# Hybrid stage re-laid: two sets of recurrence buffers, clamp as Relu, grouped ScalarE functions, output blocks in another order

## The reference, cut to what matters

```
x : 1 x 256 tokens x 1024 float32, two layers
per layer i:  h += 0.5 * SwiGLU_1(RMSNorm(h))          # d_ff 2816
              h += Mixer_i(RMSNorm(h))                 # layer 0: hybrid, layer 1: differential attention
              h += 0.5 * SwiGLU_2(RMSNorm(h))
hybrid: z, xbc, dt, gate, x_b = split(hn @ hyb_w_in)
  SSD:  xbc = silu(conv4(xbc));  dt = softplus(dt + bias);  cs = cumsum(dt * a) in chunks of 128
        y = sum_j (C_i.B_j) exp(cs_i - cs_j) dt_j x_j  (j <= i) + state of the chunk before + d * x
        y = rms_norm_in_2_groups(y * silu(z))
  LRU:  xb = conv4(x_b);  r = sigmoid(xb @ w_ra + b);  i = sigmoid(xb @ w_ix + b)
        a = exp(-8 r softplus(-lambda));  h_t = a h_(t-1) + sqrt(1 - a^2) i xb;  out = gelu(gate) * h
  h += concat(y, out) @ hyb_w_out
attention: q, k, v = split(hn @ w_qkv); rope; softmax(q1 k1) - lam softmax(q2 k2); per-head norm; @ w_o
```

## Time and profile before

| | |
|---|---|
| median of 3 runs | 1081.09 us (1081.01 to 1081.24) |
| the profiled execution's own time | 1081.11 us |
| its span, first to last instruction | 1079.3 us |
| mean granted TensorE clock | 0.988 |
| PE busy | 1054.2 us (98%) |
| PEld busy | 949.0 us (88%) |
| DVE busy | 807.9 us (75%) |
| ACT busy | 614.2 us (57%) |
| POOL busy | 69.2 us (6%) |
| hybrid stage (first input block to the next stage's first block) | 195.84 to 395.86 us of the span |
| attention stage | 765.3 to 885.2 us of the span |

### The profile page before, as it was taken

The page is one execution under the profiler, slowest core; times in us unless marked ns, Lnnn a source line. Parts: engine busy times, 40 slices in busy tenths (PEclk is TensorE's granted clock), DMA queues, the critical chain, the costliest instruction groups (busy, mean ns, idle before and its releaser), DMA issues. The chain is left out here.

```text
span 1079.3 us, 18474 instructions
## 1 busy us (share of the span) xinstructions
PE 1054.2 (98%) x6669; PEld 949.0 (88%) x6669; DVE 807.9 (75%) x1141; ACT 614.2 (57%) x982; POOL 69.2 (6%) x80
## 2 busy tenths in 40 slices
PE   9999999998988999999999999999999999999997
PEld 8888888897888998888888888888989998888886
DVE  6888775799898758888656888766689578888753
ACT  6555543676887555555534555544455756555541
POOL 0200011100131000000011000002100000000021
PEclk9999999998988999999999999999999999999999
DMA  9866676556443656667764666775475437666671
GB/s 253 215 192 190 197 215 170 141 152 204 117 123 102 178 160 191 194 193 209 195 189 142 190 190 191 222 195 166 120 203 158 126 100 213 192 189 196 190 206 39
DMA packets 365602, 189.07 MB, mean 175 GB/s; under 512 B 5840, under 2 KB 364512, under 8 KB 365552
## 3 DMA queue, kind: packets, MB, share of 16 engines
q1 hardware_dynamic: 365296, 187.84, 61.6%
q0 software_dynamic: 256, 0.59, 0.3%
HBM read 186.81 MB, written 1.06 MB: 174 GB/s over the span
## 5 line engine op out<-in xcount | busy, mean ns | idle before, releaser
L190 DVE TENSOR_TENSOR wlo<-raw,whi 128x1024 fp32r<-128x1024 f32 (+1 forms) x324 | 419.8, 1315 | 67.9 <-ACT whi L185 66.3
L185 ACT ACTIVATE whi<-raw 128x1024 fp32r<-128x1024 f32 (+1 forms) x322 | 352.1, 1114 | 26.5 <-PE psum L205 19.9
L217 PE MATMUL psum<-xn,whi 128*128 128x512 f32 x1408 | 354.4, 393 | 0.1
L217 PEld LDWEIGHTS psum<-xn,whi 128*128 128x128 f32 x1408 | 253.5, 189 | 45.9 <-DVE xn L302 0.4
L220 PEld LDWEIGHTS psum<-xn,wlo 128*128 128x128 f32 x1408 | 192.4, 190 | 13.8
L220 PE MATMUL psum<-xn,wlo 128*128 128x256 f32 x1408 | 196.9, 282 | 0.0
L217 PE MATMUL psum<-hid,whi 128*128 128x512 f32 x704 | 171.8, 391 | 0.0
L217 PEld LDWEIGHTS psum<-hid,whi 128*128 128x128 f32 x704 | 128.1, 189 | 24.0
L201 PE MATMUL psum<-xn,whi 128*128 128x256 f32 x480 | 124.1, 295 | 0.7 <-ACT arena L1530 0.7
L202 PE MATMUL psum<-xn,whi 128*128 128x256 f32 x480 | 121.2, 288 | 0.0
L505 ACT ACTIVATE arena<-arena 128x256 f32<-128x256 f32 x88 | 36.9, 420 | 112.1 <-DVE arena L558 112.1
(11 more groups left out here) (218 smaller groups left out, 913.6 us busy)
## 6 DMA issues: line engine op xcount, KB each, us to landing
raw<-in_ffn_gate SPq DMA_DIRECT2D x88, 512.0 KB, 3.9
raw<-in_ffn_up SPq DMA_DIRECT2D x88, 512.0 KB, 3.9
raw<-in_ffn_down SPq DMA_DIRECT2D x64, 704.0 KB, 4.6
raw<-in_hyb_w_in SPq DMA_DIRECT2D x36, 512.0 KB, 4.3
raw<-in_dif_w_qkv SPq DMA_DIRECT2D x24, 512.0 KB, 4.6
raw<-in_hyb_w_out SPq DMA_DIRECT2D x16, 512.0 KB, 4.3
raw<-in_dif_w_o SPq DMA_DIRECT2D x8, 512.0 KB, 4.3
hid<-cs_rows SPq DMA_DIRECT2D x4, 512.0 KB, 6.7
```

The costliest lines, as they stand in the source:

```text
L185: act.activation(whi[:, s, 0:k * P], raw[:, s, 0:k * P], ACT.Copy).then_inc(s_whi, 1)
L190: dve.tensor_tensor(wlo[:, s, 0:k * P], raw[:, s, 0:k * P], whi[:, s, 0:k * P].bitcast(F32), ALU.subtract).then_inc(s_wlo, 1)
L217: pe.matmul(acc, hi[:, j, :], x[:, t, :, :], start=start and j == 0, stop=False)
```

## The change

The hybrid stage and its neighbours are edited so:

- **dt** is turned to tokens first; softplus runs on 128 x 32; the cumulative sums come from TensorE (`sums_of_dt`, five matmuls against the triangle, between the two blocks of pair 5) in place of VectorE's scans. The heads' bias and a are spread by one matmul. The softplus of the LRU's lambda moves into the down products of the FFN before.
- **Decays**: ScalarE clamps (four `Relu` of 128 columns with a bias per partition) and takes one exponential of 512 columns for a pair of heads. The block off the diagonal is a product of two factors: exp(cs) goes to DRAM and back as `erows` beside `csb`, and VectorE makes two products of 128 columns from it. `exponents` is gone; `decay_products` on the diagonal has 512 columns.
- **LRU** has two sets of buffers (the second in the place of the gates' weights and of xbc's B and C); the second half's sigmoids wait for all gate products of TensorE instead of for the scans. Functions of a kind are grouped on ScalarE. The scans of both halves run during the output blocks. The products on GpSimd move to VectorE (`lru_ix`, `gate_y`) and ScalarE (`square_y`).
- **x to tokens** goes in `after` 6, 7, 10, 12, on more banks; the group sums of both groups stand together after pair 16, and one `group_scales` stands between the blocks of pair 17.
- **Output** does all y blocks first and then all LRU blocks, with eight PSUM accumulators, and h is updated during the last eight blocks. The hand-over to the next stage goes by single blocks.
- VectorE no longer rounds the second block of pairs 15 and 16.
- **Attention**: the first `take_qk` comes before pair 2's rounding, lambda's exponential two steps later, and the third root before the second `output_hi`.

```diff
+        def begin_hi(act, p0, k, before, ring_full=True):
+            for b, left in zip(range(2 * p0, 2 * p0 + RING), before):
+                left(lambda: split_hi(act, b, b % RING, k, b // RING, ring_full))
...
-        lr, li, la = grid(10240, 4), grid(11264, 4), grid(12288, 4)
+        lr, li, la = (grid(10240, 4), grid(7168, 4)), (grid(11264, 4), grid(8192, 4)), (grid(12288, 4), xbc[:, 8:12, :])
...
         def gate_of(k):
...
-            return xbc[:, 8 + 2 * k:10 + 2 * k, :] if k < 2 else sz[:, 2 * k - 4:2 * k - 2, :]
+            return xtok[:, k % 2, 512 * (k // 2):512 * (k // 2) + 512].rearrange("p (m t) -> p m t", m=2)
...
-        OUT_BLOCKS = [(0, 0), (1, 0), (0, 1), (1, 1)] + [(d, q) for d in range(2, DT) for q in range(2)]
+        OUT_BLOCKS = [(d, q) for q in range(2) for d in range(DT)]
...
+        def out_sum(d):
+            return banks[(5, 7, 6, 4, 0, 1, 2, 3)[d]][:, 0:T]
...
                 if j == 18:
                     sp.wait_ge(s_cs, 1)
-                    sp.dma_start(cs_rows[:, :], cs).then_inc(s_csd, 16)
-                    sp.wait_ge(s_csd, 16)
+                    sp.dma_start(cs_rows[:, 0:T], cs).then_inc(s_csd, 16)
+                    sp.wait_ge(s_er, 1)
+                    sp.dma_start(cs_rows[:, T:T + P], dt_rows[:, 0:P]).then_inc(s_csd, 16)
+                    sp.wait_ge(s_csd, 32)
                 if j in (18, 20, 22, 24):
                     q = (j - 18) // 2
-                    rows = cs_rows[4 * q:4 * q + 4, :].unsqueeze(0).to_broadcast([P, 4, T])
...
                     sp.dma_start(csb[:, 4 * q:4 * q + 4, :], rows).then_inc(s_csb[q], 16)
+                    rows = cs_rows[4 * q:4 * q + 4, T:T + P].unsqueeze(0).to_broadcast([P, 4, P])
+                    sp.dma_start(erows[:, 4 * q:4 * q + 4, :], rows).then_inc(s_csb[q], 16)
...
+            def sums_of_dt():
+                pe.wait_ge(s_sp, 10)
+                for c in range(TC):
+                    pe.matmul(sum_rows[:, c * P:(c + 1) * P], DTA[:, c * HEADS:(c + 1) * HEADS], tri, start=True, stop=True)
+                pe.matmul(sum_tok[:, 0:2 * HEADS], tri, DTA, start=True, stop=True)
+                pe.matmul(sum_tok[:, 2 * HEADS:], tri, DTN[:, 0:HEADS], start=True, stop=False)
+                pe.matmul(sum_tok[:, 2 * HEADS:], ones, DTA[:, 0:HEADS], start=False, stop=True).then_inc(s_sums, 1)
             def c_dot_b():
...
+                mm.then_inc(s_cbp, 1)
             def x_to_tokens(g):
...
                 pe.wait_ge(s_xc, 6 + 2 * g)
-                if g >= 2:
-                    pe.wait_ge(s_xt, g - 1)
-                elif g == 1:
-                    pe.wait_ge(s_cb, 2)
+                if g == 2:
+                    pe.wait_ge(s_cb, 1)
+                    pe.wait_ge(s_cbo, 1)
+                elif g == 3:
...
                 if t == 0:
-                    pe.wait_ge(s_xt, 4)
-                if t >= 2:
-                    pe.wait_ge(s_gs, 2 * (t - 1))
-                o = banks[3 + t % 2]
+                    pe.wait_ge(s_cs, 1)
+                    pe.wait_ge(s_xt, 1)
+                elif t == 2:
+                    pe.wait_ge(s_xt, 2)
+                    pe.wait_ge(s_tok, 1)
...
+                    pe.wait_ge(s_gs, 2 * (t - 3))
+                o = banks[GATE_BANK[t % 4]]
...
             def group_sums(g):
...
             after = {s: [] for s in range(18)}
-            after[0] += [dt_product]
+            middle = {s: [] for s in range(18)}
+            after[0] += [dt_product, rows_of_heads]
+            after[2] += [dt_to_tokens]
+            middle[5] += [sums_of_dt]
             after[5] += [c_dot_b]
-            after[6] += [rows_to_tokens]
-            for g, s in enumerate((6, 7, 7, 8)):
+            for g, s in enumerate((6, 7, 10, 12)):
                 after[s] += [lambda g=g: x_to_tokens(g)]
             for m in range(8):
                 after[8 + m] += [lambda m=m: head_y(2 * m), lambda m=m: head_y(2 * m + 1)]
-            for k, s in enumerate((9, 10, 13, 14)):
+            for k, s in enumerate((9, 10, 12, 13)):
                 after[s] += [lambda k=k: lru_gates(2 * k), lambda k=k: lru_gates(2 * k + 1)]
-            after[14] += [lambda: group_sums(0)]
-            after[16] += [lambda: group_scale(0)]
-            after[16] += [lambda: group_sums(1)]
-            after[17] += [lambda: group_scale(1)]
+            after[16] += [lambda: group_sums(0), lambda: group_sums(1)]
+            middle[17] += [group_scales]
             for j in range(18):
                 read_out(pe, p0 + j - 2)
                 for m in range(2):
...
                 pe.wait_ge(s_ylo if t < 8 else s_blo, t % 8 + 1)
             for k, (d, q) in enumerate(OUT_BLOCKS):
-                if q == 0:
-                    read_out(pe, p0 + 16 + d)
+                if q == 0 and d in (4, 5):
+                    read_out(pe, p0 + 12 + d)
                 b = 2 * (p0 + 18) + k
-                multiply(pe, b, b % RING, DT, hid, 8 * q, half(p0 + 18 + d, 0), start=q == 0, stop=q == 1,
+                multiply(pe, b, b % RING, DT, hid, 8 * q, out_sum(d), start=q == 0, stop=q == 1,
                          need=ready if d == 0 else None)
...
+            def take_sums():
+                act.wait_ge(s_sums, 1)
+                act.activation(cs, sum_rows, ACT.Copy).then_inc(s_cs, 1)
+                act.activation(tok[:, 2 * HEADS:], sum_tok, ACT.Copy).then_inc(s_tok, 1)
+            def factors():
+                act.activation(dt_rows[:, 0:P], sum_rows[:, P:T], ACT.Exp).then_inc(s_er, 1)
+                act.wait_ge(s_tok, 1)
...
+            def decay(m):
+                act.wait_ge(s_csb[m // 2], 32)
+                act.wait_ge(s_tok, 1)
+                if m >= 2:
+                    act.wait_ge(s_y, 2 * m - 2)
+                if m == 5:
+                    act.wait_ge(s_tap, 3 * (NX + NL))
+                v = seg_pair(m)
+                for q in range(2):
+                    hd = 2 * m + q
+                    for c in range(TC):
+                        act.activation(v[:, q, 2 * P * c:2 * P * c + P], csb[:, hd, c * P:(c + 1) * P], ACT.Relu, scale=-1.0,
+                                       bias=tok[:, 32 + 16 * c + hd:33 + 16 * c + hd]).then_inc(s_seg, 1)
+                act.wait_ge(s_seg, 4 * m + 4)
+                d = diagonal(v)
+                act.activation(d, d, ACT.Exp, scale=-1.0).then_inc(s_dec, 1)
...
                 if t == 4:
-                    act.wait_ge(s_hl, 4)
-                o = banks[3 + t % 2]
...
-            todo[17] += [lambda: gelu(0), lambda: group_rms(0)]
-            todo[18] += [lambda: group_rms(1), lambda: mult_of_lru(1), lambda: gelu(1)]
-            todo[18] += [lambda: lru_hi(0)] + [lambda t=t: y_hi(t) for t in range(4)]
+            todo[3] += [softplus_exp]
+            todo[4] += [softplus_ln]
+            todo[7] += [take_cb_off]
+            for j in range(6):
+                todo[max(j + 3, 4)] += [lambda j=j: conv_silu(j)]
+            todo[6] += [take_sums]
+            todo[6] += [factors]
+            for m in range(8):
+                todo[8 + m] += [lambda m=m: decay(m)]
+            todo[12] += [lambda t=t: gates(t) for t in range(4)]
+            todo[13] += [lambda: decays_of_lru(0)]
+            todo[14] += [lambda t=t: gates(t) for t in range(4, 8)]
+            todo[15] += [lambda: decays_of_lru(1)]
+            todo[16] += [lambda: silu_z(0), lambda: silu_z(1)]
+            todo[17] += [lambda k=k: square_y(k) for k in range(4)]
+            todo[18] += [group_rms, lambda: mult_of_lru(0), lambda: mult_of_lru(1)]
+            todo[18] += [lambda t=t: y_hi(t) for t in range(4)]
             todo[19] += [lambda t=t: y_hi(t) for t in range(4, 8)]
-            todo[19] += [lambda: lru_hi(1), lambda: gelu(2), lambda: gelu(3)]
...
-            return [lambda: residual_hi(act, n + 1, DT - 2), lambda: residual_hi(act, n + 1, DT - 1)]
+            def left(d):
+                def work(split):
+                    split()
+                    residual_hi(act, n + 1, d)
+                return work
+            for d in range(4):
+                b = 2 * (p0 + 24) + d
+                left(d)(lambda: split_hi(act, b, b % RING, DT, b // RING))
...
             def decay_products(m):
-                dve.wait_ge(s_dec, 2 * m + 2)
-                v = seg_pair(m)
-                dve.tensor_tensor(v, v, cbm[:, m // 4, :].unsqueeze(1).to_broadcast([P, 2, 3 * P]),
-                                  ALU.mult).then_inc(s_m, 1)
+                dve.wait_ge(s_dec, m + 1)
+                if m == 0:
+                    dve.wait_ge(s_cb, 1)
+                    dve.wait_ge(s_cbo, 1)
+                    dve.wait_ge(s_tok, 2)
+                dve.wait_ge(s_csb[m // 2], 32)
+                v, c = seg_pair(m), cbm[:, m // 4, :]
+                d = diagonal(v)
+                both_ = c.rearrange("p (c t) -> p c t", c=3)[:, 0:3:2, :].unsqueeze(1).to_broadcast([P, 2, 2, P])
```

(43 more changed lines are left out.)

550 lines of the change are left out of this document (290 added, 260 removed).

## The result

The changed kernel takes 1068.49 us (median; 1065.55 to 1068.67) against 1081.16 for the kernel before beside it: ratio 0.9876, 95% interval 0.9862 to 0.989. The forecast was 1064.6, its range 1058 to 1073. The profiled execution of after is the shortest, 1065.55 with a span of 1063.7 and a mean granted clock of 0.995; the three others took 1068.41 to 1068.67 at 0.992.

A forecast was written before the change was run, and what follows sets the result against it. With PE busy 98% of the span, time could come only from TensorE's work, idle gaps and slow matmuls. Terms: -22.6 + 1.0 + 1.3 + 2.2 + 3.2 + 0.4 - 2.0 = -16.5, from 1081.11 to 1064.6 us; range 1058 to 1073.

The forecast's parts named there:

- Stalls, -22.6: Hybrid: TensorE's stalls and the slow stretches after them, laid to late VectorE and GpSimd's products, all go: 22.6 us less.
- Work on TensorE, +1.0: Hybrid: spreading matmul, transposes and matmuls for the sums, less five transposes gone, add 1.0 us; bounds 0.5 and 2.
- Wait before the sums, +1.3: Before the group sums, TensorE waits 1.3 us for the squares because ScalarE is late from step 14; bounds 0 and 5.
- First output block, +2.2: After pair 17: norms and lo parts behind one scale make the first output block 2.2 us late; bounds 0.5 and 4.
- Clock, +3.2: Around pair 17: low clock slows 32 one-column products and a block, 1.1 + 2.1 us; bounds 0 and 6.
- Hand-over, +0.4: End of the hybrid: ScalarE's rounding makes the last xn tile 0.4 us late for TensorE; bounds 0 and 2.
- ScalarE's table loads: Hybrid: grouping functions saves some seven of 20 table loads at 1.28 us each, 9 us of ScalarE's time.
- Attention, -2.0: Attention: waits at L201 (0.7) and L1385 (1.1) go, L1442 loses 0.2 to 0.3; bounds -0.5 and -2.5.
- B: Rival: squares in time and clock high around pair 17, so 1.3 and 3.2 fall away: 1060.1 us; chance 0.22.
- C: Rival: ScalarE bounds from step 12, clamps at 0.40, pairs 15 and 16 wait for rounding: 1070 to 1073; chance 0.2.
- D: Rival: VectorE as late as before, stalls stay, gain only in attention and from GpSimd: 1074 to 1079; chance 0.04.
- E: Rival: SP's two-fold wait at block 18 holds up all loads, making it slower: 1083 or more; chance 0.04.

The follow-up runs named there:

- the repeat: The changed kernel run once more, unedited: 1065.67 us (1065.17 to 1066.27), ratio 0.9855.
- the added load: Changed kernel with the turns of x back after pairs 6, 7, 7, 8, plus ten VectorE operations nobody reads in steps 4 to 7: 1070.18 us.
- one moved line: Changed kernel with silu of z moved on ScalarE from step 16 to 14, ahead of the second half's gates: 1062.66 us, ratio 0.9831.

## Why the prediction came out as it did

**Right in sign and size, and in most of the mechanism.** The signs named ahead are in the profile: no wait at the third turns, POOL's row nearly empty in the hybrid (1.58, two operations of the norm before it), 1.1 before the one-column products, 1.3 at the first output block (2 forecast), low clock between; hybrid 186.97 (185.5 forecast), attention 117.12 (118). One of the signs against it is there too, in small: 0.54 at the rounding of pair 16. The profiled execution, 1065.55, and the repeat's median, 1065.67, lie 1.0 above the forecast; the first median, 1068.49, 3.9, of which 2.8 go with a lower clock in executions without a profile. That the profile is only 1.0 off is in part luck: the misses below are 1.7 for TensorE's work (with the stalls at the full 22.6), 1.2 not foreseen and 0.1 at the hand-over against 0.9 too much at the first output block, 0.2 before the sums and 0.9 in attention.

Term by term:

- *Stalls, -22.6*: all gone, and the size was right. Before, TensorE's idle time in the stage was 200.02 - 186.66 = 13.4. Of its busy 18.64 at the lower level 44 to 50% was lost, 8.2 to 9.3 (a matmul of a block starts 0.213 after the one before it there, 0.120 at the upper level; a one-column product 0.213, against 0.112). Together that is 21.6 to 22.7. The reason given for the early stall (L795) was too small in its number and half wrong in its parts. In the window 207 to 256 VectorE lost some 7.3 for dt (one reciprocal of 16 x 256 alone takes 1.74, as the added load shows again with 1.73) and 2.0 for lambda against 2.6 new, 6.7 net; the sum had 4 + 2 - 2. The moved turns, counted as a second reason, were not needed. For the later stalls the prediction blamed GpSimd, and that step failed for the first of them: at 296 us (2.6) VectorE waited for ScalarE, and the stall stayed at 2.45 when the products had left GpSimd. Its products did cost VectorE 10.4 us, about 3.4 of it between 298.8 and 306 ahead of the stall at 306.61 (7.4 for the operations L1118, L1112 and L190 that take 4.1 undisturbed), but the run that removed only that was slower. In the change all of it left together, and which part would have done is not separated.
- *Work on TensorE, +1.0*: too small, about at its bound of 2. TensorE's busy time less what the lower level cost is 186.66 less 8.2 to 9.3 before, and 183.30 less 3.2 after, so 1.6 to 2.8 us of work were added. What is left over from the stage's 13.05 when all other terms are taken off, with the stalls at the full 22.6, is 2.7.
- *Wait before the sums, +1.3*: 1.12, by the chain that was written out (20.8 us from the load at 299.86 to the end of the second square, where 21.0 was reckoned); the run with silu ahead of the gates removes it.
- *First output block, +2.2*: 1.31. The eight norms, eight lo parts and the copy take 6.5 (331.48 to 337.98 on VectorE) where 6.9 was reckoned; the other 0.5 is not separated.
- *Clock, +3.2*: the 32 products 5.17 for 3.49 and the block 4.50 for 2.95 (from start to start, against the run with silu ahead of the gates): 3.2. The sum is right, its parts (1.1 and 2.1) are not; that it hangs on the wait is not shown, see below.
- *Hand-over, +0.4*: 0.46.
- *Not foreseen*: 0.36 and 0.54 for ScalarE's rounding in pairs 4 and 16 and 0.34 for a lo part, 1.2 together. Pair 4's stands behind two table loads in a row (softplus, then the convolution's silu); the sum looked at ScalarE only from step 12.
- *ScalarE's table loads*: 14 in the hybrid instead of 20, where some seven were to go; nothing in the sum hangs on the one.
- *Attention, -2.0*: 2.87, 0.4 beyond its bound. L1385's and L201's waits went as said (1.1 and 0.7); the root's move took 0.7 off L1442 instead of 0.2 to 0.3.

The rivals: B (squares in time, clock high) is what one moved line makes of the kernel: 1061.5 in the profiled execution, which has no low stretch, and 1062.7 by the median, instead of the 1060.1 it was priced at. C was half there: the lateness on ScalarE is real and reached pair 16's rounding, but the clamps ran at 0.33 each (1.31 for four) as in the forecast, not 0.40. D did not occur. E's path was there in small: `csb` came 0.6 us late for ScalarE at 249.80, and ScalarE then waited 4.1 us in five pieces for weight loads; none of it reached TensorE.

**Open.** The executions with the silu ahead have a mean clock of 0.994 to 0.998, those of the changed kernel and its variants without it 0.990 to 0.997. All seven profiles of the latter have a low stretch around pair 17; of the four with the silu ahead, two have none in the hybrid. So the wait seems to make it likelier, which is not shown: the stretch was absent after an idle 2.59 in one run and present with no wait ahead of the products in another. What decides it in one execution is not settled.
